# Two token blocks enter the first FFN unnormalised; loads, block sizes and the norms ahead of the mixers change with it

## The reference, cut to what matters

```
def _rmsnorm(x, g):
    y = x * lax.rsqrt(jnp.mean(x * x, axis=-1, keepdims=True) + EPS) * g

def _swiglu(h, w_gate, w_up, w_down):
    return (jax.nn.silu(h @ w_gate) * (h @ w_up)) @ w_down

layer 0: x += 0.5 * swiglu(rmsnorm(x));  x += even mixer(rmsnorm(x));  x += 0.5 * swiglu(rmsnorm(x))
layer 1: x += 0.5 * swiglu(rmsnorm(x));  x += odd mixer(rmsnorm(x));   x += 0.5 * swiglu(rmsnorm(x))
y = rmsnorm(x)
```

## Time and profile before

| what | value |
|---|---|
| median of 3 runs | 2370.59 us (2370.56 to 2372.8) |
| the profiled execution: its time | 2370.56 us |
| its span on the slowest core (core 2) | 2368.8 us, 2365.2 to 2368.8 over the cores |
| granted TensorE clock, all cores | 0.992 of full speed |
| PE busy | 97% of the span |
| DVE, ACT, POOL busy | 42%, 23%, 9% |

### The profile page before, as it was taken

How to read it: one execution, slowest core, us unless ns; L and a number is a source line. 1 busy time by engine, 2 the same in 40 slices (tenths; PEclk the granted TensorE clock), 3 DMA queues, 4 the chain that set the end, 5 groups by cost and what they waited for, 6 DMA issues and landing times.

```text
span 2368.8 us, 33471 instructions; the slowest of 8 cores (2365.2 to 2368.8 us)
## 1 busy us (share of the span) xinstructions
PE 2303.5 (97%) x12455; PEld 1217.9 (51%) x12455; DVE 998.5 (42%) x1689; ACT 546.4 (23%) x993; POOL 204.5 (9%) x248
## 2 busy tenths in 40 slices
PE   5999999999999999999999999999989999999996
PEld 2455555554455555555554555555544555555553
DVE  4552232267568342232284422322687724223226
ACT  4401101145234201101242011011434410110123
POOL 1000000065100000000000000000510000000014
PEclk9999999999999999999999999999999999999998
DMA  8141121101321041221110311111032113111103
GB/s 200 45 74 35 37 38 38 38 9 28 65 50 32 1 79 37 37 38 38 36 27 7 67 36 36 36 36 37 19 89 53 32 30 56 36 36 36 36 1 151
DMA packets 21037, 107.37 MB, mean 45 GB/s; under 512 B 3984, under 2 KB 6032, under 8 KB 11152
## 3 DMA queue, kind: packets, MB, share of 16 engines
q0 software_dynamic: 11952, 80.75, 19.1%
q1 hardware_dynamic: 8928, 24.49, 3.0%
HBM read 174.89 MB, written 11.08 MB: 79 GB/s over the span
## 4 chain that ended last, share of the span: by engine, by line
PE 91%; DVE 4%; DMA 2%; issue 1%; ACT 1%; POOL 0%; DVEq 0%; ACTq 0%; SPq 0%; POOLq 0%
PE ps L435 88%; PE ps L430 2%; DVE scr L1009 1%; DMA xT<-x 1%; DMA ws<-wall 0%; DVE xT L680 0%; DVE hT L619 0%; DVE hT L607 0%; DVE xT L607 0%; PE ps L567 0%; DVE mid L1014 0%; ACT L577 0%; DVE nrm L493 0%; DVE scr L1024 0%; POOL accr L535 0%
## 5 line engine op out<-in xcount | busy, mean ns | idle before, releaser
L435 PE MATMUL ps<-hT,ws 128*128 128x512 bf16 (+2 forms) x7680 | 1424.7, 348 | 3.6 <-ACT mid L987 1.8
L435 PEld LDWEIGHTS ps<-hT,ws 128*128 128x128 bf16 x7680 | 751.4, 98 | 668.9 <-issue 13.6
L435 PE MATMUL ps<-mid,ws 128*128 128x512 bf16 (+2 forms) x4160 | 771.2, 347 | 0.0
L667 DVE TENSOR_TENSOR mid<-ps,scr 128x512 bf16<-128x512 f32 (+2 forms) x440 | 268.7, 611 | 929.9 <-PE ps L435 890.7
L435 PEld LDWEIGHTS ps<-mid,ws 128*128 128x128 bf16 x4160 | 405.0, 98 | 359.2 <-issue 5.1
L662 ACT ACTIVATE scr<-ps 128x512 f32<-128x512 f32 (+2 forms) x440 | 234.0, 533 | 1407.5 <-PE ps L435 1364.4
L680 DVE SCALAR_TENSOR_TENSOR xT<-ps,xT 128x512 f32<-128x512 f32 (+2 forms) x480 | 289.7, 610 | 283.4 <-PE ps L435 283.3
L385 POOL DMA_DIRECT2D ws<-wall x83 | 44.3, 536 | 1978.6 <-PE ps L435 1966.8
L619 DVE SCALAR_TENSOR_TENSOR hT<-xT,misc,nrm 128x512 bf16<-128x512 f32 (+2 forms) x157 | 100.9, 682 | 18.2 <-ACT nrm L591 18.2
L430 PE MATMUL ps<-hT,ws 128*128 128x512 bf16 (+2 forms) x320 | 66.3, 358 | 6.8 <-DVE hT L619 6.7
L484 ACT ACTIVATE nrm<-xT 128x512 f32<-128x512 f32 (+2 forms) x86 | 47.2, 560 | 56.1 <-DVE xT L917 35.5
(11 more groups left out here) (89 smaller groups left out, 518.4 us busy)
## 6 DMA issues: line engine op xcount, KB each, us to landing
ws<-wall POOLq DMA_DIRECT2D x65, 1024.0 KB, 8.8
ws<-wall POOLq DMA_DIRECT2D x12, 768.0 KB, 9.7
xT<-x SPq DMA_DIRECT2D x6, 1024.0 KB, 9.7
y<-xT SPq DMA_DIRECT2D x4, 1024.0 KB, 3.9
ws<-wall POOLq DMA_DIRECT2D x6, 512.0 KB, 16.1
y<-xT SPq DMA_DIRECT2D x4, 512.0 KB, 2.7
xT<-x SPq DMA_DIRECT2D x2, 768.0 KB, 8.7
y<-xT SPq DMA_DIRECT2D x2, 768.0 KB, 3.3
```

Source lines behind the costliest of these rows:

```text
L435: ins = e.matmul(banks[bk][:, 0:n], l, rr, start=(i == 0), stop=(i == len(pairs) - 1))
L667: P.add("dve", lambda e: e.tensor_tensor(out=mcol(fs, a, a + n), in0=banks[ku][:, 0:n], in1=s_(0, n), op=ALU.mult), r=[("ps", ku), s_.key( ...
```

## The change

**Start.** The constants are loaded first. Block 0 of x comes in four pieces of two chunks (`XPER`) by SP's queue; the first weights, blocks 1 and 2 of x and the weights between them are issued one after another by POOL's queue with no wait for x. DVE writes bf16(x*g) into `hT` (`raw_in`), and PE multiplies it by gate and up weights (`raw`). What leaves PSUM is multiplied by 1/rms: the gate on DVE ahead of the SiLU, the product on POOL behind the multiply (`raw_out`). This holds for the 12 cells of blocks 0 and 1 in the first part. Their proper h, which the later parts use, are made afterwards (`finish_h`). Block 0 has eight stat matmuls, block 1 two (`quad`), block 2 one (`line`).

**Blocks.** 512, 384, 512, 384, 384 tokens.

**Norms 1, 4 and 6.** `heavy` is gone: four stat matmuls per block (`groups` 4), each for a pair of chunks that DVE adds; 1/rms stays in SBUF; five of the eight h are POOL multiplies followed by an ACT copy with g, and three are DVE's.

**Odd mixer.** No windows are held back.

**y.** Four chunks per store for blocks 0 to 3; only block 4 goes in pairs.

```
-BL = [(0, 512), (512, 512), (1024, 384), (1408, 512), (1920, 256)]
+BL = [(0, 512), (512, 384), (896, 512), (1408, 384), (1792, 384)]
+XPER = [2, 4, 4, 4, 4]
...
-        return dram(y_out, b, c0, c1, 2 if b >= NB - 2 else 4)
+        return dram(y_out, b, c0, c1, 2 if b == NB - 1 else 4)
...
-            P.add("dve" if i == end and b == NB - 1 else "pool", lambda e: e.tensor_tensor(out=o, in0=acc(0, n), in1=q(0, n), op=ALU.add),
...
-            if self.heavy:
-                P.add("act", lambda e: e.activation(out=banks[bk][:, 0:n], in_=q(0, n), func=AF.Exp, scale=-0.5),
...
-            if self.heavy and c not in self.split[b]:
-                P.add("dve", lambda e: e.scalar_tensor_tensor(out=dst, in0=xs(b, c), scalar=g, in1=banks[bk][:, 0:n], op0=ALU.mult, op1=ALU.mult),
...
+        def raw(b, f, chunks, held=None):
+            for c in chunks:
+                for bk, o in ((kg, base + c * 128), (ku, base + 1024 + c * 128)):
+                    P.add("pe", lambda e, bk=bk, o=o, c=c: e.matmul(banks[bk][:, 0:n], wt(o, o + 128), hs(b, c), start=c == 0, stop=c == NCH - 1),
...
+            def gate():
+                P.add("dve", lambda e: e.tensor_tensor(out=s_(0, n), in0=banks[kg][:, 0:n], in1=q(0, n), op=ALU.mult),
...
+            def silu():
+                P.add("act", lambda e: e.activation(out=s_(0, n), in_=s_(0, n), func=AF.Silu), r=[s_.key(0, n)], w=[s_.key(0, n)])
+            def mul():
+                P.add("dve", lambda e: e.tensor_tensor(out=s_(0, n), in0=banks[ku][:, 0:n], in1=s_(0, n), op=ALU.mult),
...
+                P.add("pool", lambda e: e.tensor_tensor(out=mcol(f, a, a + n), in0=s_(0, n), in1=q(0, n), op=ALU.mult),
...
+        def raw_in(b, c):
+            P.add("dve", lambda e: e.tensor_scalar(out=hs(b, c), in0=xs(b, c), scalar1=g, scalar2=None, op0=ALU.mult),
...
+            for b, f in ((0, 3), (1, 2), (1, 3), (0, 4), (1, 4), (0, 5), (1, 5)):
+                held = raw(b, f, range(4))
+                if (b, f) == (1, 4):
+                    nm0.stat(2, 0, 0, 1)
...
-            if di < 2 and not started:
-                waiting.append(window)
...
-    load_x(0, 0)
-    load_x(0, 4)
...
+    for c in range(0, NCH, 2):
+        load_x("sp", 0, c)
+    load_item(0, (0, 2048))
+    load_item(0, (2048, 4096))
+    load_item(1, (0, 2048))
+    load_x("pool", 1, 0)
+    load_x("pool", 1, 4)
+    load_item(1, (2048, 4096))
+    load_x("pool", 2, 0)
+    load_x("pool", 2, 4)
+    load_item(2, (0, 2048))
+    load_item(2, (2048, 4096))
...
+    cells = [(2, 0), finish_h(0), (2, 1), first(3), (2, 2), (2, 3), (2, 4), (2, 5), lambda: load_item(3),
+             (3, 0), finish_h(1), first(4)] + [(3, f) for f in range(1, 6)] + [(4, f) for f in range(6)] + [even_consts, odd_consts]
+    most = (0, 2, 3, 5, 6)
+    ffn(0, 0, Norm(1, groups=4, split=most), cells=cells, mid_hook=even_bias)
```

More of the change, by code:

```diff
@@ L350, in build_program @@
     rs = [NRM.f32(6144 + 2048 * i, 512) for i in range(2)]
+    rs0 = [R.f32(7 * T * 2 + 2048 * i, 512) for i in range(2)]
     cT = MI.f32(0, 76)
@@ L366, in build_program, with load_item @@
     slot_of = {}
-    def load_item(j, after=()):
+    def load_item(j, part=None):
         key, n = ITEMS[j]
@@ L375, in load_item @@
         src = wall[base:base + 128 * n].rearrange("(p m) -> p m", p=128)
-        pieces = [(0, 2048), (2048, 4096)] if j < 3 else [(0, n)]
-        for lo, hi in pieces:
+        for lo, hi in [part] if part else [(0, n)]:
             P.label = f"load {key}"
@@ L508, in build_program, with direct @@
         pair_wait = 6
-        def heavy_chunk(self, b, c, i):
+        def direct(self, b, c):
             n = BL[b][1]
[L513 to L522, removed]
-                return
[L524 to L533, removed]
+            P.label = f"norm{self.nidx} sq"
+            P.add("act", lambda e: e.activation(out=accr_t[c % 3][:, 0:n], in_=xs(b, c), func=AF.Square), r=[xk(b, c)], w=[("accr", c % 3)])
@@ L540, in prescale, with quad_stat @@
+        def quad_stat(self, b, gi):
+            self.stat(b, gi, gi, 2)
         def prescale(self, b, c):
@@ L556, in stat @@
             n = BL[b][1]
[L557 to L564, removed]
+            bk = 7
             P.label = f"norm{self.nidx} stat"
@@ L567, in stat @@
             P.add("pe", lambda e: e.matmul(banks[bk][:, 0:n], ones_t[:], accr_t[k][:, 0:n], start=first, stop=last),
-                  r=[("accr", k), ("ones",)], w=[("ps", bk), rk])
+                  r=[("accr", k), ("ones",)], w=[("ps", bk)])
             if not last:
                 return
[L571 to L575, removed]
+            if self.nidx == 0 and b < 2:
+                q = rs0[b]
+            else:
+                k2 = pc["rs"] % 2
+                pc["rs"] += 1
+                q = rs[k2]
+                while any(x[2] == k2 for x in hq):
+                    hq.pop(0)[1]()
             P.label = f"norm{self.nidx} rs"
@@ L578, in stat @@
                   r=[("ps", bk)], w=[q.key(0, n)])
-            if self.heavy:
-                P.add("act", lambda e: e.activation(out=banks[bk][:, 0:n], in_=q(0, n), func=AF.Exp, scale=-0.5),
[L581 to L590, removed]
             P.add("act", lambda e: e.activation(out=q(0, n), in_=q(0, n), func=AF.Exp, scale=-0.5),
                   r=[q.key(0, n)], w=[q.key(0, n)])
+            if self.nidx == 0 and b < 2:
+                return
             self.done.add(b)
@@ L694, in ffn @@
                 js = [item(("gu", l, w, f)) for f in fs]
+                js0.extend(js)
+                if cells is not None:
+                    start()
                 if cells is None:
@@ L1228, in from_blocks @@
     for b, (a, n) in enumerate(BL):
-        per = 2 if b >= NB - 2 else 4
+        per = 2 if b == NB - 1 else 4
         for c in range(0, NCH, per):
```

246 lines of the change are left out of this document (156 added, 90 removed).

## The result

The changed kernel takes 2405.6 us where the one before takes 2370.6 beside it: a ratio of 1.0146, with a 95% interval of 1.0126 to 1.0166. That is 35 us slower, outside the range of the prediction. The profiled execution has a span of 2403.7 us on its slowest core, against 2368.8.

What follows compares the result with a forecast made beforehand. PE, busy 97% of the span, was taken as the bound. Start -5.0, stat matmuls +8.0, odd mixer -7.5, tail -3.0, even mixer 0 and DVE beside POOL +9 sum to +1.5: 2372 us, range 2360 to 2382.

Steps and rivals of the forecast that it cites:

- the wait term of the start: First cells: PE waits 3 us for each of blocks 2, 3, 4 and 3 for block 1, 12 in all.
- The low clock stays: Slower rival, start: PE stays at half clock beyond the first cell, 3.5 us per further cell; three give 2382; chance 0.12.
- the term of the stat matmuls: Norms 1, 4 and 6: 60 stat matmuls at 0.23 or 0.17 us each, on PE's path, cost +8.0 us.
- DVE beside POOL: Start, odd mixer and tail: POOL multiplies meeting DVE on SBUF cost DVE about 1.0 us each, together +9.
- The 3 of the start: Start: of 12 POOL multiplies half meet something, and half of those lie on PE's path, +3 us.
- DVE becomes the bound of the last down projections: Slower rival: POOL multiplies hold DVE up; at three per block 2380, at all five about 2410; chance 0.20.
- the odd mixer: Odd mixer: windows start earlier on DVE, its bound, -7.5 us; meetings with POOL's h there cost +5.
- Covered up to the 9.7 us: Odd mixer: PE meets the last block's h later, hidden up to the 9.7 us by which PE is short of DVE.
- the tail: Stores of y after the last matmul: fewer, larger ones give -3.0 us; meetings of DVE and POOL cost +1.
- the turns of the two queues: Start: x and weights queues alternate packet by packet, so block 0 is complete at about 21.9, without it at 14.3.

Runs made afterwards that it cites:

- early-h run: The changed kernel with norm 0 of blocks 2, 3 and 4 begun earlier in the order, proper h of blocks 0 and 1 later: 2392.6 us.
- fourfold run: The kernel before with each stat matmul of norms 1, 4 and 6 issued four times, 42 more: 2375.9 us, 1.0024.
- two different edits: The changed kernel with the last block's stat matmuls given their own PSUM bank (2400.4 us), or put off by two more groups of eight matmuls (2400.6 us).
- two runs that add: The changed kernel with old norms and held-back windows, 2380.9 us; the kernel before with the changed norms and no windows held back, 2395.6 us.
- last run: The changed kernel with norm 0 earlier, last block's stat matmuls later, windows held back, POOL's h (norms 1, 4, last norm's first four blocks) on DVE: 2381.9 us.

## Why the prediction was wrong

**Wrong, the wait term of the start: "I take 3 for each and another 3 for block 1's first cells, 12 in all".** Up to the end of cell (0,0) the working held: 26.43 against 25. But the first cells of blocks 2, 3 and 4, each with the slower cells next to it, lost 6.9, 6.5 and 5.3, 18.7 where 9 was taken. Of these 8.8 are the waits for one h after another; the rest is single matmuls and the half clock behind them. Block 1's cells and their neighbours lost some 10 where 3 was taken: a wait of 3.10 for the second half of block 1's x*g, which stand in DVE's list behind the sums of the first half's squares, one of 2.90 for block 2's sum of squares, and low clock beside them (0.86 and 0.81 from 26.4 to 45.2). No run takes these two away.

I misread the row that I leaned on, 6.7 in 7 waits. The seven lie in the first cells of blocks 0 and 1 (4.9 and 1.8); those of blocks 2 to 4 had no wait at all, since their h had been begun several cells ahead, as the timeline of PE before shows for blocks 2 and 3:

```profile
72.49 2.76 PE L430 MATMUL ps<-hT,ws 128*128 128x384 bf16 x16
...
97.01 3.62 PE L430 MATMUL ps<-hT,ws 128*128 128x512 bf16 x16
```

I hadn't asked how far ahead the new order begins them. The early-h run gives 13 back, so the place in the order is shown as the cause for blocks 2 to 4. "The low clock stays" was a rival of mine for the first cells; the low clock came, but later, behind the late h.

**Wrong, the term of the stat matmuls: "with no wait of PE around them", +8.0.** The three norm stages cost 24.0. The own time isn't what failed: it is 0.18 by the changed kernel's rows for 384 tokens, and 0.24 for 512 in the fourfold run. What I hadn't seen is that the last block's first stat matmul follows the block before with nothing between, onto the same bank, while Ln, which must read the bank first, stands behind the last block's squares: waits of 3.59, 3.57 and 3.23 (the longest of each norm) and a half-clock stretch behind two of them. Without that wait the three stages are 13.0 and 12.7 shorter, by two different edits, so it is shown as the cause of about half of the 24.0. But the whole time falls by only 5, not by 11 to 14, because the next links of the chain are as late and the mixers and the tail wait for them. Shown besides: the norms' part as a whole (two runs that add). What is left in the last run, 4 to 5 us per norm stage over the old norms, fits the own time of 15 more stat matmuls (some 3 by the rows) and waits; I have not taken it apart further, and the lower rate at which h are let out may have a part in it and in the late h of the mixers.

**Half right, DVE beside POOL, +9.** Meetings happen as priced: a scan of 512 tokens took 1.88 and 2.02 instead of 1.22 where the last block's POOL multiplies ran, in the timeline of DVE:

```profile
1756.98 1.88 DVE L1091 TENSOR_TENSOR_SCAN scr<-scr 128x512 f32<-128x512 f32 x1
...
1761.23 2.02 DVE L1091 TENSOR_TENSOR_SCAN scr<-mid 128x512 f32<-128x512 f32 x1
```

The rule of the Trainium skill ("SBUF — State Buffer", Who interferes with whom), by which such a pair of instructions exclude each other, agrees with these rows. But without POOL's h ahead of the mixers the time fell by 1.3 to 3.4 only, and in the even mixer, which I had put at 0; the odd mixer, where I had put 5 of the 9, didn't change. The 3 of the start were not taken apart. The rival that DVE becomes the bound of the last down projections fell; that its estimate, about 2410, lies near the measured time is chance, for PE waited there for Ln (11.8 in all) and 1.6 for DVE's pair sums.

**Right in sum, by luck, the odd mixer.** -7.5 + 5 = -2.5 was forecast and -1.2 measured. The first window did start early, 2.8 us after the mixer begins (forecast 2.6). But neither term came out: with the windows held back the stretch is only 1.1 longer, and without POOL's h 0.2 shorter. "Covered up to the 9.7 us" held: PE waited 8.5 for the last block's h behind the windows, and taking that wait away gave nothing. The wait then stands at the windows' end, which fits a stretch bound by DVE's work; that is argued, no run shortens DVE's windows.

**Right in sign, the tail.** -2 with its meeting, -4.2 measured. By the sizes and stores alone it is -1.3; the rest comes from PE's own late end, for the tail is counted from there. Block 3's first store is issued 2.1 us before PE's last bf16 matmul ends, with sizes and stores alone 3.0 after it; and in the two runs that shorten PE's last wait the tail is 20.4 and 19.8.

**Right, the turns of the two queues.** DVE took up block 0's fourth piece at 23.27 (forecast landed at 21.9; the pieces came 5.1 to 5.2 us apart, forecast 4.4 to 4.8), and with the weights held back at 15.85.

## What to carry to other kernels

When a change rewrites an order by hand, ask for each late consumer how many matmuls stand between the start of its chain and its first use, and compare this with the chain's length, in the last norm 3.6 us from the start of the last residual add (2386.64) to the end of 1/rms (2390.28); a wait price from another order doesn't carry over. Look in the new order for two instructions that stand side by side and write the same bank with a reader on another engine between them, and then for what stands ahead of that reader in its own engine's list. And when a wait is removed and only a part of the time comes back, look for the next link of the same chain before calling the first one the cause.

## What the runs showed of the hardware

In three stretches in which PE was fed one matmul at a time the granted clock fell (0.70, 0.71 and 0.81 in the windows above), and the late h there cost 18.7 where the waits themselves are 8.8. It doesn't always fall. In the early-h run block 4's first cell is fed in the same way for a shorter time, and its window is (same columns as above):

```profile
108.70:113.20 4.50, 3.19 (x18) 1.49 (x16) 3.73 (x7) 0.49 (x1) 0.00 (x0) 1.00 0.00 0
```

And behind two waits of nearly the same length in the changed kernel, 3.59 in norm 1 and 3.57 in norm 4, the clock differs:

```profile
543.10:545.60 2.50, 2.50 (x18) 1.52 (x17) 1.92 (x2) 0.37 (x2) 2.12 (x2) 1.00 0.00 0
1748.40:1752.20 3.80, 3.80 (x16) 1.92 (x16) 2.02 (x2) 1.29 (x3) 2.39 (x3) 0.65 0.00 0
```

Stat matmuls show 0.4 to 0.6 us of busy time each in the trace, but keep PE from its next work for only 0.18 (384 tokens, single) to 0.24 (512 tokens, back to back), and 42 more of them lengthened the whole kernel by 5.6, or 0.13 each. Even DVE's smallest operations are held up beside POOL: 16 columns took 0.98 and 0.86 us at 1764.53 and 1765.61 in the odd mixer, and 0.17 at 1759.57, with no POOL multiply beside it.
